# Triangular inverse in one group of eight matrices on VectorE and TensorE, in place of two groups of four

## The chip, the cores and the metric

The kernel runs on one core of a Trainium2 chip. TensorE (PE in the profile) does matrix products into PSUM, VectorE (DVE) and ScalarE (ACT) work on SBUF and PSUM, and the queue of SyncE (SP) loads weights. The metric is the device time of one execution in microseconds; the time before is the median of three runs.

## What is computed

The program is two layers of a hybrid decoder trunk on 256 tokens of 1024 channels: four parallel head groups (gated linear recurrence, gated DeltaNet, RG-LRU, RWKV-7), then cross-attention and a feed-forward part, which is SwiGLU in the first layer and eight experts in the second. The change touches the DeltaNet and RWKV groups alone. Each of them needs, once a layer, the inverses of unit triangular matrices that couple the tokens of a chunk. The kernel takes chunks of 128 tokens, so that with 4 heads and 256 tokens there are eight matrices of 128x128. For DeltaNet the reference has this system (with chunks of 64); for RWKV-7 it is the same kind of system, hidden in a scan over tokens:

```python
def chunk_gated_delta(q, k, v, g, beta):
    """S_t = exp(g_t)(I - b_t k_t k_t^T) S_{t-1} + b_t k_t v_t^T ; o_t = S_t^T q_t.
    q,k (B,H,S,dk), v (B,H,S,dv), g,beta (B,H,S)."""
    ...
    lower = jnp.einsum("bhntd,bhnsd->bhnts", kb, kc) * rel * strict
    rhs = jnp.concatenate([vc * bc[..., None], kb * jnp.exp(gc)[..., None]], axis=-1)
    uw = lax.linalg.triangular_solve(jnp.eye(CHUNK, dtype=f32) + lower, rhs,
                                     left_side=True, lower=True, unit_diagonal=True)
    ...
def rwkv7_scan(r, w, k, v, kk, a):
    """S_t = S_{t-1}(diag(w_t) - kk_t^T (a_t*kk_t)) + v_t^T k_t ; y_t = S_t r_t.  inputs (B,S,H,d)."""
```

## The kernel before

The program is written engine by engine: each engine has its own list of instructions, and semaphores (`wait_ge`, `then_inc`) are the only order between the lists. Each VectorE operation also waits for the one before it (`Chain`). `inverse(i)` stands once in VectorE's list and once in TensorE's. It runs four times: i = 0 (DeltaNet) and i = 1 (RWKV) in the first layer, i = 2 and 3 in the second. N holds the eight matrices side by side, 1024 columns. X and Y hold only their diagonal blocks of 64x64: the upper one on the first 64 partitions and the lower one on the others (`HALVES`), so that the eight matrices take 8 x 64 = 512 columns.

The inverse is built by doubling, in `LEVELS` = 7 levels v = 0 to 6. N is the triangular matrix, X its inverse so far and Y the transpose of X. In each level TensorE multiplies N and X into PSUM (T below), VectorE masks the result to the blocks of that level (T1), TensorE multiplies T1 with Y in both orders (P below), and VectorE subtracts the two from X and Y. Level 0 needs no P; level 5 keeps the upper half of the new Y in the columns from 512 on; level 6 makes the block that joins the two diagonal ones, with one product for each matrix where the levels below have two. The last copy of level 6 releases `solve`.

Before the change the eight matrices are handled as two groups of four (g = 0 and 1). Each group has its own PSUM banks (g, 2 + g, 4 + g) and its own counts on the semaphores `inv_t`, `inv_t1`, `inv_p` and `inv_xy`, whose target values come from `done_xy` and `done_p`.

Between the steps of a level other work is called by `after(v)`. On VectorE, in i = 0 and 2, this is `rwkv_ahead`: it prepares operands of the RWKV group at levels 0, 1, 3, 5 and 6 and stands between T1 and X. In i = 1 and 3 VectorE has no such work. On TensorE it is half of a memory-token projection (`kv`) at levels 0 and 1, one more product in i = 0 at level 1, and 8 transposes at level 3 in i = 1 (`turn_operands`); it stands behind P of its level.

All VectorE operations of a kind are recorded at the line of their helper: L812 for `tt`, L815 for `ts`, L1101 for the copy. TensorE's `mm` is L1462.

Of the kernel before, what the change touches and what calls it, by code (L numbers as in the profile page):

```python
# [103 lines left out]
def build(nc, A, out):  # L104
# [14 lines left out]
    with ExitStack() as ctx:  # L119
# [146 lines left out]
        def done_p(i, v, g, y):  # L266
            return (4 * LEVELS - 6) * i + 4 * (v - 1) + (2 * g + y + 1 if v < LEVELS - 1 else g + 1)
# [538 lines left out]
        def _(dve):  # L806
# [261 lines left out]
            def inverse(i, after=None):  # L1068


                N, X, Y, T1 = mt(3), mt(4), mt(5), mt(0)
                for v in range(LEVELS):
                    for g in range(2):
                        s_ = slice(256 * g, 256 * g + 256)
                        dve.wait_ge(S("inv_t"), 2 * (LEVELS * i + v) + g + 1)
                        if v == 0:
                            tt(many(T1[:, s_]), many(ps[:, g, 0:256]), rep(flip_b(0), 4), ALU.mult)
                            tt(many(X[:, s_]), rep(ident_b[:, :], 4), many(T1[:, s_]), ALU.subtract).then_inc(S("inv_xy"), 1)
                            for u in HALVES:
                                tt(many(T1[u, s_]), many(N[u, 512 * g:512 * g + 512])[:, :, u], rep(lvl(0)[u, u], 4), ALU.mult)  # L1080
                            tt(many(Y[:, s_]), rep(ident_b[:, :], 4), many(T1[:, s_]), ALU.subtract).then_inc(S("inv_xy"), 1)
                        elif v < LEVELS - 1:
                            tt(many(T1[:, s_]), many(ps[:, g, 0:256]), rep(flip_b(v), 4), ALU.mult).then_inc(S("inv_t1"), 1)
                        else:
                            ts(T1[HD:P, s_], ps[HD:P, g, 0:256], -1.0, ALU.mult).then_inc(S("inv_t1"), 1)
                    if after:
                        after(v)
                    if v:
                        for g in range(2):
                            s_ = slice(256 * g, 256 * g + 256)  # L1090
                            if v < LEVELS - 1:
# [366 lines left out]
        def _(pe):  # L1458
# [197 lines left out]
            def inverse(i, after=None):  # L1656
# [458 lines left out]
```

## Time and profile before

| what | value |
|---|---|
| median of 3 runs | 2117.27 us (2116.48 to 2118.86) |
| the profiled execution | 2117.68 us, span 2115.8 us |
| TensorE busy | 1922.4 us, 91% |
| VectorE busy | 1480.4 us, 70%, 1565 instructions |
| ScalarE busy | 1143.3 us, 54% |
| granted TensorE clock, mean | 0.941 |

The busy shares are means over stages with very different limits. The four inverses lie at about 205 to 244, 269 to 301, 830 to 869 and 894 to 928 us from the start of the span. In a timeline a row stands for one instruction or a run of like ones: its start, the time it covers, engine, line, operands, count, and in brackets how long the engine had been idle and what released it.

### The profile page before, as it was taken

To read this page: it belongs to the slowest core of one execution; us is meant where nothing else is said; L and a number is where in the kernel's file an instruction comes from. 1 tells how busy PE (TensorE), PEld (TensorE's weight loads), DVE (VectorE), ACT (ScalarE), POOL (GpSimd) and SP (SyncE) were. 2 spreads that over 40 slices of the span, in tenths; PEclk is the share of its full clock that TensorE was granted. 3 is DMA by queue.
4 is the path that set the end of the run, shared out by engine and by line. 5 is a ranking of instruction groups with operands and counts; after the bars stand their busy time and mean duration, and the time that the engine had idled before them with its cause. 6 is when DMAs were issued, how large, how long until landed. Compare 5 with 4: busy or idle time off the path is not lost.

```text
span 2115.8 us, 28844 instructions
## 1 busy us (share of the span) xinstructions
PE 1922.4 (91%) x12072; PEld 1637.5 (77%) x12073; DVE 1480.4 (70%) x1565; ACT 1143.3 (54%) x1078; POOL 0.2 (0%) x4
## 2 busy tenths in 40 slices
PE   6987789889998987789869999999999999999996
PEld 6975677779997966578748888888888888888884
DVE  6776544354447686535369888889888898988885
ACT  5543304343434643214357777767777776777773
POOL 0000000000000000000000000000000000000000
PEclk9997789989998998789979999999999999999998
DMA  7531003235554530003249999999999999999992
GB/s 227 173 127 40 22 22 113 86 114 189 193 193 123 179 102 22 20 22 120 80 157 384 346 358 338 378 334 368 355 337 364 333 387 328 369 357 340 358 374 83
DMA packets 238774, 466.06 MB, mean 220 GB/s; under 512 B 11056, under 2 KB 87088, under 8 KB 238640
## 3 DMA queue, kind: packets, MB, share of 16 engines
q1 hardware_dynamic: 238640, 464.16, 61.8%
q8 instruction: 97, 1.59, 0.3%
q14 instruction: 37, 0.30, 0.0%
HBM read 463.09 MB, written 1.05 MB: 219 GB/s over the span
## 4 chain that ended last, share of the span: by engine, by line
PE 83%; DVE 12%; ACT 3%; issue 2%; DVEq 0%; DMA 0%; ACTq 0%
PE ps L1887 29%; PE ps L1477 16%; PE ps L1897 14%; PE ps L1462 11%; PE ps L1495 7%; DVE MT L812 4%; PE ps L1943 1%; PE ps L1957 1%; PE ps L1918 1%; PE ps L1465 1%; DVE MT L815 1%; DVE hT_lo L818 1%; DVE TMP L812 1%; DVE MT L1032 1%; DVE MT L818 1%
## 5 line engine op out<-in xcount | busy, mean ns | idle before, releaser
L1253 DVE TENSOR_TENSOR wlo<-raw,whi 128x2048 fp32r<-128x2048 f32 x140 | 320.2, 2290 | 70.7 <-ACT whi L694 70.6
L694 ACT ACTIVATE whi<-raw 128x2048 fp32r<-128x2048 f32 x140 | 268.8, 1921 | 130.8 <-PE ps L1897 77.6
L825 DVE TENSOR_TENSOR wlo<-raw,whi 128x2048 fp32r<-128x2048 f32 x85 | 194.5, 2289 | 131.8 <-ACT whi L429 131.7
L1253 DVE TENSOR_TENSOR wlo<-PT,whi 128x2048 fp32r<-128x2048 f32 x84 | 192.1, 2291 | 33.6 <-ACT whi L694 33.6
L429 ACT ACTIVATE whi<-raw 128x2048 fp32r<-128x2048 f32 x85 | 161.9, 1905 | 55.9 <-PE ps L1495 46.7
L1887 PE MATMUL ps<-whi,hE_hi 128*128 128x512 f32 x672 | 185.4, 398 | 2.4 <-DVE hE_lo L1319 2.4
L694 ACT ACTIVATE whi<-PT 128x2048 fp32r<-128x2048 f32 x84 | 161.4, 1922 | 34.7 <-PE ps L1887 34.0
L1887 PE MATMUL ps<-wlo,hE_hi 128*128 128x512 f32 x672 | 180.1, 390 | 0.0
L1887 PE MATMUL ps<-whi,hE_lo 128*128 128x512 f32 x672 | 179.8, 389 | 0.0
L1477 PE MATMUL ps<-hT_hi,whi 128*128 128x256 f32 x928 | 136.3, 291 | 23.2 <-DVE hT_lo L818 23.2
L1887 PEld LDWEIGHTS ps<-wlo,hE_hi 128*128 128x128 f32 x672 | 126.2, 188 | 27.1
L1887 PEld LDWEIGHTS ps<-whi,hE_lo 128*128 128x128 f32 x672 | 126.2, 188 | 26.7
L1477 PEld LDWEIGHTS ps<-hT_hi,whi 128*128 128x128 f32 x928 | 124.8, 199 | 25.8 <-DVE hT_lo L818 24.9
L1887 PEld LDWEIGHTS ps<-whi,hE_hi 128*128 128x128 f32 x672 | 122.0, 188 | 24.8 <-DVE hE_lo L1319 2.6
L1897 PE MATMUL ps<-whi,act_hi 128*128 128x512 f32 x336 | 133.8, 398 | 1.4 <-DVE act_lo L1297 1.4
L1477 PE MATMUL ps<-hT_hi,wlo 128*128 128x256 f32 x928 | 134.2, 289 | 0.0
L1477 PE MATMUL ps<-hT_lo,whi 128*128 128x256 f32 x928 | 133.1, 287 | 0.0
L1897 PE MATMUL ps<-whi,act_lo 128*128 128x512 f32 x336 | 131.0, 390 | 0.0
L1897 PE MATMUL ps<-wlo,act_hi 128*128 128x512 f32 x336 | 130.7, 389 | 0.0
L1477 PEld LDWEIGHTS ps<-hT_hi,wlo 128*128 128x128 f32 x928 | 123.7, 198 | 0.0
L1477 PEld LDWEIGHTS ps<-hT_lo,whi 128*128 128x128 f32 x928 | 122.8, 197 | 0.0
L1462 PE MATMUL ps<-MT 64*64 64x64 f32 (+1 forms) x2272 | 90.4, 227 | 26.3 <-DVE MT L812 20.4
(259 smaller groups left out, 3313.9 us busy)
## 6 DMA issues: line engine op xcount, KB each, us to landing
raw<-in_moe_w_up SPq DMA_DIRECT2D x111, 1024.0 KB, 6.8
PT<-in_moe_w_down SPq DMA_DIRECT2D x56, 1024.0 KB, 6.5
PT<-in_moe_w_gate SPq DMA_DIRECT2D x55, 1024.0 KB, 6.7
TMP<-in_moe_w_gate SPq DMA_DIRECT2D x55, 1024.0 KB, 6.7
raw<-in_moe_w_down SPq DMA_DIRECT2D x55, 1024.0 KB, 6.4
raw<-in_w_in SPq DMA_DIRECT2D x28, 1024.0 KB, 5.5
raw<-in_ffn_w_gate SPq DMA_DIRECT2D x11, 1024.0 KB, 5.3
raw<-in_ffn_w_up SPq DMA_DIRECT2D x11, 1024.0 KB, 5.4
```

The lines of the kernel that those rows point to most:

```text
L429: nc.scalar.activation(whi[i % SPL][:, :], raw[d % RAW][:, :], ACT.Copy).then_inc(S("w_hi"), 1)
L694: nc.scalar.activation(ex_hi[m % XSPL], ex_raw[m % XRAW], ACT.Copy).then_inc(S("w_hi"), 1)
L812: return chain.link(lambda: V.tensor_tensor(o, x0, x1, op))
L815: return chain.link(lambda: V.tensor_scalar(o, x0, s1, s2, op0, op1) if op1 else V.tensor_scalar(o, x0, s1, None, op0))
L818: return chain.link(lambda: V.scalar_tensor_tensor(out=o, in0=x0, scalar=s_, in1=x1, op0=op0, op1=op1))
L825: V.tensor_tensor(wlo[i % SPL][:, :], raw[d % RAW][:, :], whi[i % SPL][:, :].bitcast(F32), ALU.subtract).then_inc(S("w_lo"), 1)
L1253: V.tensor_tensor(ex_lo[m % XSPL], ex_raw[m % XRAW], ex_hi[m % XSPL].bitcast(F32), ALU.subtract).then_inc(S("w_lo"), 1)
L1462: return Signalled(pe.matmul(o, lhsT, rhs, start=start, stop=stop, skip_group_check=True))
L1477: ins = pe.matmul(ps[:, bank, SEQ * m:SEQ * m + SEQ], wp[a_][:, k, P * m:P * m + P], src[b_][:, k, :], start=i == 0 and k == 0, stop=last)
L1495: ins = pe.matmul(ps[:, 4 + 2 * t + hf, :], src(b_, kk, t), wp[a_][:, kk, 512 * hf:512 * hf + 512], start=first and kk == 0 and i == 0, st ...
L1887: ins = pe.matmul(ps[:, bank, :], h_[b_][:, X_K * i + k, :], wp[a_][:, k, :], start=i == 0 and n_ == 0 and k == 0, stop=i == 1 and n_ == 2 ...
L1897: ins = pe.matmul(ps[:, 4 + hf, :], act_[b_][:, P * (TM_ROWS * i + kk):P * (TM_ROWS * i + kk) + P], wp[a_][:, kk, 512 * hf:512 * hf + 512] ...
```

## The change

The two groups become one. VectorE handles all eight matrices in one operation: 128x512 elements where there were two of 128x256. TensorE makes a product for all eight matrices before it signals, 16 matmuls of the program where it was 8 (at level 6, 8 where it was 4). The trace shows each of these fp32 matmuls as two. Banks 1, 3 and 5 are no longer used by the inverse, and the counts of the semaphores are halved. The number of matmuls is the same. Nothing else is touched.

```diff
-        def done_xy(i, v, g, y):
-            return (4 * LEVELS - 2) * i + 4 * v + (2 * g + y + 1 if v < LEVELS - 1 else g + 1)
+        def done_xy(i, v, y):
+            return (2 * LEVELS - 1) * i + 2 * v + (y + 1 if v < LEVELS - 1 else 1)
...
+                eight = lambda m: many(m[:, 0:512], 8)
                 for v in range(LEVELS):
-                    for g in range(2):
-                        s_ = slice(256 * g, 256 * g + 256)
-                        dve.wait_ge(S("inv_t"), 2 * (LEVELS * i + v) + g + 1)
-                        if v == 0:
-                            tt(many(T1[:, s_]), many(ps[:, g, 0:256]), rep(flip_b(0), 4), ALU.mult)
...
-                        elif v < LEVELS - 1:
-                            tt(many(T1[:, s_]), many(ps[:, g, 0:256]), rep(flip_b(v), 4), ALU.mult).then_inc(S("inv_t1"), 1)
-                        else:
-                            ts(T1[HD:P, s_], ps[HD:P, g, 0:256], -1.0, ALU.mult).then_inc(S("inv_t1"), 1)
+                    dve.wait_ge(S("inv_t"), LEVELS * i + v + 1)
+                    if v == 0:
+                        tt(eight(T1), many(ps[:, 0, :], 8), rep(flip_b(0), 8), ALU.mult)
...
+                    elif v < LEVELS - 1:
+                        tt(eight(T1), many(ps[:, 0, :], 8), rep(flip_b(v), 8), ALU.mult).then_inc(S("inv_t1"), 1)
+                    else:
+                        ts(T1[HD:P, 0:512], ps[HD:P, 0, :], -1.0, ALU.mult).then_inc(S("inv_t1"), 1)
                     if after:
                         after(v)
                     if v:
-                        for g in range(2):
-                            s_ = slice(256 * g, 256 * g + 256)
-                            if v < LEVELS - 1:
-                                dve.wait_ge(S("inv_p"), done_p(i, v, g, 0))
-                                tt(X[:, s_], X[:, s_], ps[:, 2 + g, 0:256], ALU.subtract).then_inc(S("inv_xy"), 1)
-                            dve.wait_ge(S("inv_p"), done_p(i, v, g, 1))
-                            if v < LEVELS - 2:
-                                tt(Y[:, s_], Y[:, s_], ps[:, 4 + g, 0:256], ALU.subtract).then_inc(S("inv_xy"), 1)
...
+                        if v < LEVELS - 1:
+                            dve.wait_ge(S("inv_p"), done_p(i, v, 0))
+                            tt(X[:, 0:512], X[:, 0:512], ps[:, 2, :], ALU.subtract).then_inc(S("inv_xy"), 1)
+                        dve.wait_ge(S("inv_p"), done_p(i, v, 1))
+                        if v < LEVELS - 2:
+                            tt(Y[:, 0:512], Y[:, 0:512], ps[:, 4, :], ALU.subtract).then_inc(S("inv_xy"), 1)
...
                 for v in range(LEVELS - 1):
-                    for g in range(2):
...
-                        if v:
-                            pe.wait_ge(S("inv_xy"), done_xy(i, v - 1, g, 0))
-                        blocks(g, n_, x_ if v else (lambda u, k: ident[u, u]), g).then_inc(S("inv_t"), 1)
                     if v:
-                        for g in range(2):
...
-                            pe.wait_ge(S("inv_xy"), done_xy(i, v - 1, g, 1))
-                            pe.wait_ge(S("inv_t1"), 2 * ((LEVELS - 1) * i + v - 1) + g + 1)
-                            blocks(2 + g, y_, t_, g).then_inc(S("inv_p"), 1)
-                            blocks(4 + g, t_, y_, g).then_inc(S("inv_p"), 1)
+                        pe.wait_ge(S("inv_xy"), done_xy(i, v - 1, 0))
+                    blocks(0, n_, x_ if v else (lambda u, k: ident[u, u])).then_inc(S("inv_t"), 1)
+                    if v:
+                        pe.wait_ge(S("inv_xy"), done_xy(i, v - 1, 1))
+                        pe.wait_ge(S("inv_t1"), (LEVELS - 1) * i + v)
+                        blocks(2, y_, t_).then_inc(S("inv_p"), 1)
+                        blocks(4, t_, y_).then_inc(S("inv_p"), 1)
```

On VectorE, in i = 1 at level 1 and the start of level 2, the list was this before (con16b is the mask, so a row with it is T1; MT,ps rows are X and Y, and inv_t, inv_p are the signals of T and P):

```order
L812 TENSOR_TENSOR MT<-ps,con16b 128x256 [waits inv_xy,inv_t]
L812 TENSOR_TENSOR MT<-ps,con16b 128x256 [waits inv_t1,inv_t]
L812 TENSOR_TENSOR MT<-MT,ps 128x256 [waits inv_t1,inv_p]
L812 TENSOR_TENSOR MT<-MT,ps 128x256 [waits inv_xy,inv_p] x3
L812 TENSOR_TENSOR MT<-ps,con16b 128x256 [waits inv_xy,inv_t]
L812 TENSOR_TENSOR MT<-ps,con16b 128x256 [waits inv_t1,inv_t]
L812 TENSOR_TENSOR MT<-MT,ps 128x256 [waits inv_t1,inv_p]
```

and is this now:

```order
L812 TENSOR_TENSOR MT<-ps,con16b 128x512 [waits inv_xy,inv_t]
L812 TENSOR_TENSOR MT<-MT,ps 128x512 [waits inv_t1,inv_p]
L812 TENSOR_TENSOR MT<-MT,ps 128x512 [waits inv_xy,inv_p]
L812 TENSOR_TENSOR MT<-ps,con16b 128x512 [waits inv_xy,inv_t]
L812 TENSOR_TENSOR MT<-MT,ps 128x512 [waits inv_t1,inv_p]
```

A level had six operations and has three, and each now waits for the signal of the whole product.

On TensorE, in i = 0 at level 3, the rows before are the T products of the two groups (8 matmuls each, of which the first waits) and then P of the two groups (16 each):

```order
L1462 MATMUL ps<-MT 64x64 [waits inv_xy]
L1462 MATMUL ps<-MT 64x64 x7
L1462 MATMUL ps<-MT 64x64 [waits inv_xy]
L1462 MATMUL ps<-MT 64x64 x7
L1462 MATMUL ps<-MT 64x64 [waits inv_t1,inv_xy]
L1462 MATMUL ps<-MT 64x64 x15
L1462 MATMUL ps<-MT 64x64 [waits inv_t1,inv_xy]
L1462 MATMUL ps<-MT 64x64 x15
```

and now:

```order
L1459 MATMUL ps<-MT 64x64 [waits inv_xy]
L1459 MATMUL ps<-MT 64x64 x15
L1459 MATMUL ps<-MT 64x64 [waits inv_t1,inv_xy]
L1459 MATMUL ps<-MT 64x64 x31
```

The four starts became two: one run of 16 for T and one of 32 for P. The products of a second group, which stood between a group's T and its P, are gone.

On VectorE at the end of i = 0, levels 5 and 6 before `rwkv_ahead`(6), the list was:

```order
L812 TENSOR_TENSOR MT<-MT,ps 128x256 [waits dve_step,inv_p]
L812 TENSOR_TENSOR MT<-MT,ps 64x256 [waits inv_xy,inv_p]
L812 TENSOR_TENSOR MT<-MT,ps 64x256 [waits dve_step]
L812 TENSOR_TENSOR MT<-MT,ps 128x256 [waits inv_xy,inv_p]
L812 TENSOR_TENSOR MT<-MT,ps 64x256 [waits inv_xy,inv_p]
L812 TENSOR_TENSOR MT<-MT,ps 64x256 [waits dve_step]
L815 TENSOR_SCALAR MT<-ps 64x256 [waits inv_xy,inv_t]
L815 TENSOR_SCALAR MT<-ps 64x256 [waits inv_t1,inv_t]
```

and is now:

```order
L812 TENSOR_TENSOR MT<-MT,ps 128x512 [waits dve_step,inv_p]
L812 TENSOR_TENSOR MT<-MT,ps 64x512 [waits inv_xy,inv_p]
L812 TENSOR_TENSOR MT<-MT,ps 64x512 [waits dve_step]
L815 TENSOR_SCALAR MT<-ps 64x512 [waits inv_xy,inv_t]
```

Eight operations became four; X comes first in both, and T1 of level 6 (L815) last.

## Rows read from the trace of the kernel before

**Rows 1.** The page: busy time and share of the span by engine; chain that ended last.
```profile
PE 1922.4 (91%) x12072; PEld 1637.5 (77%) x12073; DVE 1480.4 (70%) x1565; ACT 1143.3 (54%) x1078; POOL 0.2 (0%) x4
...
PE 83%; DVE 12%; ACT 3%; issue 2%; DVEq 0%; DMA 0%; ACTq 0%
```

**Rows 2.** Windows of i = 0 and i = 1: length, busy us of each engine, clock.
```profile
205.50:244.40 38.90, 29.24 (x578) 25.66 (x578) 31.75 (x71) 11.97 (x24) 0.00 (x0) 0.90 0.09 29
269.40:301.40 32.00, 28.84 (x584) 25.64 (x584) 20.64 (x47) 1.79 (x3) 0.00 (x0) 0.95 0.11 36
```

**Rows 3.** Timeline of i = 1, levels 1 and 2: start, duration, what, idle before.
```profile
276.07 1.15 PE L1462 MATMUL ps<-MT 64*64 64x64 f32 x32
276.80 0.95 DVE L812 TENSOR_TENSOR MT<-ps,con16b 128x256 f32<-128x256 f32 x2 [1.37 <-PE ps L1462]
...
277.37 2.08 PE L1462 MATMUL ps<-MT 64*64 64x64 f32 x64 [0.15 <-DVE MT L812]
...
283.03 1.15 PE L1462 MATMUL ps<-MT 64*64 64x64 f32 x32
...
284.33 3.01 PE L1462 MATMUL ps<-MT 64*64 64x64 f32 x96 [0.15 <-DVE MT L812]
```

**Rows 4.** Chain of waits in i = 1, level 4: start, duration, what.
```profile
292.06 0.70 PE ps L1462 x16
...
292.78 0.43 DVE MT L812
...
294.88 0.44 DVE MT L812
295.32 0.14 issue
295.45 0.70 PE ps L1462 x16
```

**Rows 5.** Groups of VectorE instructions by shape: busy us, mean ns | idle.
```profile
L812 DVE TENSOR_TENSOR MT<-MT,ps 128x256 f32<-128x256 f32 x72 | 30.3, 421 | 12.5 <-PE ps L1462 6.2 <-DVE MT L812 0.5
...
L812 DVE TENSOR_TENSOR MT<-MT,ps 128x512 f32<-128x512 f32 x11 | 7.6, 688 | 82.2 <-PE ps L1477 82.2
...
L812 DVE TENSOR_TENSOR MT<-ps,con 128x512 f32<-128x512 f32 x4 | 2.8, 691 | 0.9 <-PE ps L1462 0.7
```

**Rows 6.** Timeline of i = 1, P(6) and the first products of `solve`.
```profile
299.75 1.18 PE L1462 MATMUL ps<-MT 64*64 64x64 f32 x16 [0.93 <-DVE MT L815]
...
301.44 1.97 PE L1462 MATMUL ps<-TMP,MT 128*128 128x64 f32 x8 [0.51 <-DVE MT L1101]
```

**Rows 7.** Timeline of i = 0: T(0), T(1), P(1), T(2), X(3), X(5), copies, `solve`.
```profile
205.54 1.73 PE L1462 MATMUL ps<-con,MT 64*64 64x64 f32 x32 [2.96 <-DVE MT L812]
...
211.87 1.15 PE L1462 MATMUL ps<-MT 64*64 64x64 f32 x32
...
213.29 2.08 PE L1462 MATMUL ps<-MT 64*64 64x64 f32 x64 [0.28 <-DVE MT L812]
...
219.81 1.15 PE L1462 MATMUL ps<-MT 64*64 64x64 f32 x32
...
226.51 2.00 DVE L812 TENSOR_TENSOR MT<-MT,ps 128x256 f32<-128x256 f32 x4
...
235.31 2.90 DVE L812 TENSOR_TENSOR MT<-MT,ps 128x256 f32<-128x256 f32 x6
...
243.44 0.94 DVE L1101 COPY MT<-ps 64x256 f32<-64x256 f32 x2
...
244.44 2.16 PE L1462 MATMUL ps<-TMP,MT 64*64 64x64 f32 x16 [4.37 <-DVE MT L1101]
```

**Rows 8.** Windows at the end of i = 0; the clock stands after the engines.
```profile
236.00:240.00 4.00, 2.25 (x32) 1.93 (x30) 3.48 (x8) 0.00 (x0) 0.00 (x0) 1.00 0.00 0
240.00:244.40 4.40, 0.07 (x2) 0.00 (x0) 3.93 (x10) 0.00 (x0) 0.00 (x0) 0.50 0.00 0
```

**Rows 9.** Timeline of i = 3: a pause of TensorE inside P(3).
```profile
915.28 1.15 PE L1462 MATMUL ps<-MT 64*64 64x64 f32 x31 [1.26 <-issue]
```

More of the change, by code:

```diff
@@ L261, in at_b, with done_p @@
             return par_ * 256 + t * P + c * HD
[L263 to L267 removed]
+        def done_xy(i, v, y):
+            return (2 * LEVELS - 1) * i + 2 * v + (y + 1 if v < LEVELS - 1 else 1)
+        def done_p(i, v, y):
+            return (2 * LEVELS - 3) * i + 2 * (v - 1) + (y + 1 if v < LEVELS - 1 else 1)
         def col(a, n=1):
@@ L1658, in inverse, with blocks @@
                 pe.wait_ge(S("inv_n"), i + 1)
-                def blocks(bank, lhsT, rhs, g):
-                    for k in range(4):
+                def blocks(bank, lhsT, rhs):
+                    for k in range(2 * NH):
                         for u in HALVES:
@@ L1665, in blocks @@
                     return ins
+                n_ = lambda u, k: N[u, P * k + u.start:P * k + u.stop]
+                x_ = lambda u, k: X[u, HD * k:HD * k + HD]
+                y_ = lambda u, k: Y[u, HD * k:HD * k + HD]
+                t_ = lambda u, k: T1[u, HD * k:HD * k + HD]
                 for v in range(LEVELS - 1):
-                    for g in range(2):
-                        n_ = lambda u, k: N[u, 512 * g + P * k + u.start:512 * g + P * k + u.stop]
-                        x_ = lambda u, k: X[u, 256 * g + HD * k:256 * g + HD * k + HD]
-                        if v:
-                            pe.wait_ge(S("inv_xy"), done_xy(i, v - 1, g, 0))
-                        blocks(g, n_, x_ if v else (lambda u, k: ident[u, u]), g).then_inc(S("inv_t"), 1)
@@ L1682, in inverse @@
+                    blocks(0, n_, x_ if v else (lambda u, k: ident[u, u])).then_inc(S("inv_t"), 1)
[4 more added lines that the diff above has]
+                        blocks(4, t_, y_).then_inc(S("inv_p"), 1)
                     if after:
                         after(v)
-                for g in range(2):
-                    pe.wait_ge(S("inv_xy"), done_xy(i, LEVELS - 2, g, 0))
-                    for k in range(4):
-                        mm(ps[HD:P, g, HD * k:HD * k + HD], N[0:HD, 512 * g + P * k + HD:512 * g + P * k + P],
-                           X[0:HD, 256 * g + HD * k:256 * g + HD * k + HD]).then_inc(S("inv_t"), 1 if k == 3 else 0)
@@ L1689, in inverse @@
-                for g in range(2):
-                    pe.wait_ge(S("inv_xy"), done_xy(i, LEVELS - 2, g, 1))
-                    pe.wait_ge(S("inv_t1"), 2 * ((LEVELS - 1) * i + LEVELS - 2) + g + 1)
-                    for k in range(4):
-                        s_ = slice(256 * g + HD * k, 256 * g + HD * k + HD)
-                        mm(ps[0:HD, 4 + g, HD * k:HD * k + HD], T1[HD:P, s_], Y[HD:P, s_]).then_inc(S("inv_p"), 1 if k == 3 else 0)
+                pe.wait_ge(S("inv_xy"), done_xy(i, LEVELS - 2, 0))
@@ new lines, in inverse @@
+                for k in range(2 * NH):
+                    mm(ps[HD:P, 0, HD * k:HD * k + HD], N[0:HD, P * k + HD:P * k + P],
+                       X[0:HD, HD * k:HD * k + HD]).then_inc(S("inv_t"), 1 if k == 2 * NH - 1 else 0)
+                pe.wait_ge(S("inv_xy"), done_xy(i, LEVELS - 2, 1))
+                pe.wait_ge(S("inv_t1"), (LEVELS - 1) * i + LEVELS - 1)
+                for k in range(2 * NH):
+                    s_ = slice(HD * k, HD * k + HD)
+                    mm(ps[0:HD, 4, s_], T1[HD:P, s_], Y[HD:P, s_]).then_inc(S("inv_p"), 1 if k == 2 * NH - 1 else 0)
@@ L1695, in inverse @@
                 if after:
                     after(LEVELS - 1)
[L1697 removed]
+                pe.wait_ge(S("inv_xy"), done_xy(i, LEVELS - 1, 0))
             def solve(bank, t, r_):
```

21 lines of the change are left out of this document (9 added, 12 removed).

## The prediction

> **What bounds the kernel now.** I read the busy shares and the chain of work that ended last first [rows 1]. TensorE holds 83% of the chain, VectorE 12%. That average says little about the inverse, so I asked for the busy time over the stretches of the two inverses of the first layer [rows 2]: i = 0 takes about 38.9 us, with VectorE busy for 31.75 and TensorE for 29.24; i = 1 takes about 32.0, with TensorE busy for 28.84 and VectorE for 20.64 only. The second pair, in the second layer, has the same instructions. So the four inverses are some 143 us of 2116, and in the odd ones VectorE is idle a third of the time: there its operations matter by their latency, not by their sum.
>
> Names below: T(v) are the products N·X of level v, T1(v) the VectorE operation that masks them, P(v) the two sets of products after it (first those for X, then those for Y), X(v) and Y(v) the two subtractions. A number after a colon is a start in the trace.
>
> The timeline of i = 1 shows the steps [rows 3]. T(1) starts at 276.07 with no idle time in front of it: it stood in TensorE's queue behind the memory-token products. T1(1) for the first four matrices starts 0.73 later, P(1) starts at 277.37, so T to P is 1.30. Level 2 repeats it: 283.03, again without idle time, then 284.33. The two groups overlap: while VectorE masks the first four matrices, TensorE makes the products of the other four. The trace has two matmuls for each product of the program, so a product of one group (8 blocks) is 16 matmuls. 96 in 3.01 against 32 in 1.15 give 29 ns for each, so 16 of them are 0.47 us.
>
> The chain of waits in level 4 shows the other case, with no foreign products in the way [rows 4]: P(4) at 292.06, 0.72 until X of the first group, then X, Y, X, Y at 0.525 each (292.78 to 294.88), T1 of the first group 0.44, a gap of 0.14, and P(5) at 295.45. The period is 3.39 us. T(5) is not in that chain at all: it lies under the four subtractions. The second T1 lies under the first products of P.
>
> **The change, part by part.** VectorE: an inverse had 10 operations at level 0, 6 in each of levels 1 to 4, 8 at level 5 and 4 at level 6, together 46; it has 5, 3 each, 4 and 2, together 23. That is 92 operations fewer in four inverses. A 128x256 one from PSUM takes 421 ns, a 128x512 one 688 to 691 [rows 5], so a pair of 0.84 becomes 0.69, and with the gaps 1.05 becomes 0.78. VectorE loses 92 x 0.155 = 14 us of busy time. I use 0.69 for every merged operation, since both rows at 512 columns have it, with and without a mask. No row has the bf16 mask at 512 columns, so the bounds are 0.69 and 0.84 (nothing gained over two).
>
> TensorE: the same matmuls, in runs of 32 of the trace's matmuls in place of 16. Every wait for a block now lasts 16 matmuls longer, 0.47 us: T to T1 becomes 0.73 + 0.47 = 1.20, P to X becomes 0.72 + 0.47 = 1.19.
>
> What each costs on the path:
> - T to P, where TensorE's queue sets the start of T: 1.20 + 0.69 + 0.14 = 2.03 in place of 1.30, **+0.73**. The cover that is gone is the second group's T products, under which the first T1 lay. In i = 1 this is levels 1 and 2 (memory-token products ahead) and level 4 (8 transposes ahead): 2.19 us.
> - A period with nothing foreign in it, from P(v) to P(v+1): 1.19 to X, 0.69 for X, 0.14, then T (the queue is free at 64 x 0.0294 = 1.88, so X at 2.02 decides), 1.20 to T1, 0.69, 0.14: 4.05 in place of 3.39, **+0.66**. Y(v) runs from 2.13 to 2.82, before T1 can start at 3.22: it is hidden. What was a chain of VectorE operations becomes a strict alternation of the engines. In i = 1 these are P(2) to P(3) and P(4) to P(5): 1.32 us.
> - The tail of i = 1, from P(5) at 295.45 to the first product of `solve` at 301.44 [rows 4, 6] is 5.99. After: P(5) lets X start at 1.19; the lower and upper Y (64x512, taken at 0.69 like a full one) follow at 2.13 and 2.86 and end at 3.55; the T1 of level 6 from 3.62 to 4.31 (T(6) is 16 matmuls at 65 ns, from the 16 in 1.18 of P(6) [rows 6], done by 3.3); P(6) at 4.45; the copy 1.20 later, at 5.65, 0.69 long; `solve` at 6.40: **+0.41**.
> An odd inverse therefore loses 2.19 + 1.32 + 0.41 = 3.92 us. Level 0 costs nothing there: its operations end before T(1), which the memory-token products hold back to 276.07.
>
> In i = 0 VectorE also does the work of `rwkv_ahead`, and parts of it are bound by VectorE. From [rows 7]: T(0) runs at 54 ns a matmul (32 in 1.73), so T1(0) waits 0.86 longer, and five operations of 0.73 in place of ten of 0.46 give that back. T(1) at 211.87 is set by the queue; P(1) comes 2.03 later, at 213.90 in place of 213.29. From there to T(2) TensorE is the limit (6.52 us from 213.29 to 219.81), so T(2) is at 220.42, P(2) at 222.45, P(3) at 226.50. T1(3) ends 0.14 before that; two operations of `rwkv_ahead` follow, 1.57 with their gaps: X(3) at 227.93, where it was 226.51: +1.42. From X(3) to X(5) it was 8.80. Now 0.69 + 0.14 + 1.20 + 0.69 + 0.14 = 2.86 to P(4), 4.05 to P(5), of which T1(5) ends 0.14 before, and three operations of `rwkv_ahead` with gaps, 2.31: 9.08, +0.28. From X(5) at 235.31 to `solve` at 244.44 VectorE works without a pause, 9.13. Of the inverse's ten operations in it five are left: X, Y, Y, T1 and the copy take 3.82 with their gaps, and `rwkv_ahead` 4.05 as before, 7.87 in all: -1.26. An even inverse therefore loses 1.42 + 0.28 - 1.26 = 0.44 us.
>
> The sum is 2 x (3.92 + 0.44) = 8.7 us. Everything after an inverse is a chain: `solve` waited for the last copy in both [rows 6, 7], and the chain of the whole run has no DMA share [rows 1], so I take the delay as passed on in full. The profiled execution took 2117.68 (its span is 2115.8), which gives 2126.4; against the median of 2117.27 it is 2126.0.
>
> **A rule against the rows.** The rows say that merging two operations saves 0.155 us of VectorE, and that it pays only where VectorE is the limit. The Trainium skill, "VectorE: DVE Perf Modes", section on the TRN2 errata, says that every Vector instruction pays a fixed latency and advises tiles of 512 elements or more so that it is paid once. The durations agree with it; followed alone it would take off up to the 14 us of busy time and speaks for a faster kernel. The rival of that name below is worked out from the rows.
>
> **The rivals.**
> - *VectorE stays the limit (faster).* If the next T were still hidden, a period would be two operations with gaps, T1, the gap and P to X: 0.78 + 0.78 + 0.69 + 0.14 + 1.19 = 3.58, still not under 3.39. To win, X must also start 0.72 after P: 3.11, 0.28 less. Over five levels of two odd inverses that is -2.8, with the two tails of the even ones -2.5: about 2112. The point that decides is whether T to T1 stays near 0.73 with twice the products, and [rows 3] show 29 ns a matmul, so 32 cannot be done by then. 5%.
> - *The loss is absorbed (same).* The odd loss of 3.9 passes on only if nothing later waits for something else. No DMA stands in the chain; but one stall of TensorE by its own instruction stream, 1.26 us before the products at 915.28 [rows 9], lies inside i = 3 and could vanish or fall on an idle stretch. With the stall gone (-1.3) and VectorE the limit at level 3 of the even inverses too, so that their loss of 0.44 turns into the whole gain of the tail (-1.26 each, 3.4 less for the two), it is 2121.3. 10%.
> - *The clock falls inside an inverse (slower still).* The granted clock stayed at 1.00 while TensorE was busy for 2.25 of 4.00 us, and stood at 0.50, which is 1.2 GHz, in the stretch after, in which it was idle [rows 8]. The new period leaves it busy for 2.8 of 4.05 us, a higher share than the 0.56 of that first row, so I expect no fall. If it did fall, matmuls at 54 ns [rows 7] make a period 6.3 us in place of 4.05, about 2.2 for each level until it rises: two such places in two inverses give +4 to +9, 2130 to 2135. The Trainium skill, "Perfetto Trace Analysis", section Matmul Optimizations, asks for matmuls back to back because the engine scales with use; this change takes that away in the odd inverses. 9%.
> - *The walk holds:* 76%, by itself 2122.5 to 2129.5: -1.3 for the stall, -1.2 to +1.6 for the spread of the three runs, +2 for half of the bound of 0.84 for a merged operation (two of them on the path of ten periods, 0.15 each, is 3 us).
>
> **The numbers.** The likeliest is 2126. With the stall, the spread and the two neighbours the range for 8 in 10 is 2121 to 2130.5. A measurement can tell 0.2%, 4.2 us, from no change: below 2113 is faster, above 2121.5 slower. Slower takes the walk and the clock, 85%; same 10%; faster 5%.
>
> **What would show it.** VectorE busy near 1466 in place of 1480 us; matmul count unchanged. In i = 1 the distance from P(4) to P(5) near 4.05, with VectorE idle before T1 for some 0.4 us and before X for some 0.4; T to P near 2.03; the stretch of i = 1 near 36 us and that of i = 0 near 39.3. In i = 0 `solve` should follow X(5) by 7.9. The prediction is wrong if merged operations take well over 0.69, if TensorE issues the wider blocks faster than 29 ns a matmul, or if the clock row of an inverse shows 0.5 where it was 1.0.

## The result and the profile after

| | before | after |
|---|---|---|
| median (range), 5 runs each on one chip | 2118.68 us (2116.48 to 2118.94) | 2127.07 us (2126.59 to 2128.49) |
| span of the profiled execution | 2115.8 us | 2124.7 us |
| VectorE busy | 1480.4 us, 1565 instructions | 1466.5 us, 1473 instructions |

The ratio is 1.0044, with a 95% interval from 1.0029 to 1.0059: 8.4 us slower by the medians. The forecast was 8.7 slower. In the kernel after, the helpers stand three lines higher: `mm` is L1459 and the copy L1098.

The page of after answers to [rows 1]: first the busy times, then the chain of work that ended last.

```profile
PE 1924.4 (91%) x12072; PEld 1640.7 (77%) x12073; DVE 1466.5 (69%) x1473; ACT 1143.3 (54%) x1078; POOL 0.2 (0%) x4
...
PE 85%; DVE 10%; ACT 3%; issue 1%; DVEq 0%; DMA 0%; ACTq 0%
```

VectorE lost 92 instructions and 13.9 us of work, the number of matmuls is the same, and the kernel is slower all the same. In the chain of work that ended last, VectorE's share went from 12% to 10% and TensorE's from 83% to 85%: of the blocks of matmuls that VectorE's work used to cover, more now lie on the path.

The windows of after's first two inverses, cut at their own first T(0) and first product of `solve`, answer to [rows 2] (length, busy time of each engine, clock):

```profile
203.98:243.54 39.56, 29.67 (x579) 26.31 (x579) 28.20 (x48) 11.97 (x24) 0.00 (x0) 0.89 0.09 28
268.55:304.24 35.69, 29.08 (x585) 26.18 (x585) 17.07 (x24) 1.79 (x3) 0.00 (x0) 0.93 0.10 32
```

In i = 1 VectorE does 17.07 us of work where it did 20.64, in 24 operations where it had 47. TensorE does the same work. The window is 3.7 us longer: both engines now stand idle more.

The timeline of after in i = 1 shows where (start, duration, what, idle before and its releaser). It answers to [rows 3, 4, 6]:

```profile
275.04 1.15 PE L1459 MATMUL ps<-MT 64*64 64x64 f32 x32
276.24 0.69 DVE L812 TENSOR_TENSOR MT<-ps,con16b 128x512 f32<-128x512 f32 x1 [2.08 <-PE ps L1459]
277.07 2.08 PE L1459 MATMUL ps<-MT 64*64 64x64 f32 x64 [0.89 <-DVE MT L812]
...
293.80 3.08 PE L1459 MATMUL ps<-MT 64*64 64x64 f32 x96 [0.89 <-DVE MT L812]
294.99 0.69 DVE L812 TENSOR_TENSOR MT<-MT,ps 128x512 f32<-128x512 f32 x1 [1.33 <-PE ps L1459]
295.92 0.69 DVE L812 TENSOR_TENSOR MT<-MT,ps 128x512 f32<-128x512 f32 x1 [0.25 <-PE ps L1459]
296.93 0.69 DVE L812 TENSOR_TENSOR MT<-ps,con16b 128x512 f32<-128x512 f32 x1 [0.32 <-PE ps L1459]
297.76 3.07 PE L1459 MATMUL ps<-MT 64*64 64x64 f32 x80 [0.89 <-DVE MT L812]
298.95 0.69 DVE L812 TENSOR_TENSOR MT<-MT,ps 128x512 f32<-128x512 f32 x1 [1.33 <-PE ps L1459]
...
302.24 1.22 PE L1459 MATMUL ps<-MT 64*64 64x64 f32 x16 [1.40 <-DVE MT L815]
303.50 0.68 DVE L1098 COPY MT<-ps 64x512 f32<-64x512 f32 x1 [1.41 <-PE ps L1459]
304.24 1.97 PE L1459 MATMUL ps<-TMP,MT 128*128 128x64 f32 x8 [0.78 <-DVE MT L1098]
```

Read the brackets. TensorE stands 0.89 us before each of P(1) to P(5), released by T1, where it stood 0.15 before P(1), P(2) and P(4) [rows 3] and 0.38 before P(3) and P(5). VectorE stands 0.32 us before T1, 0.25 before Y and 1.33 before X. T to P is 277.07 - 275.04 = 2.03 us (it was 1.30), the period P(4) to P(5) 3.96 (3.39), and from P(5) to `solve` 6.48 (5.99).

In i = 0 the rows of after that answer to [rows 7] are X(5) with the two Y behind it, the copy and `solve`:

```profile
235.63 2.20 DVE L812 TENSOR_TENSOR MT<-MT,ps 128x512 f32<-128x512 f32 x3
...
242.80 0.68 DVE L1098 COPY MT<-ps 64x512 f32<-64x512 f32 x1
243.54 2.16 PE L1459 MATMUL ps<-TMP,MT 64*64 64x64 f32 x16 [2.83 <-DVE MT L1098]
```

From X(5) to `solve`, 235.63 to 243.54, it is 7.91 us in place of 9.13. This is the one place that gained.

### The profile page after: what moved, and what is told of

The parts are those of the page before. It is cut to its first block, busy times and chain, and to the rows that moved or that the text cites. A ratio compares the mean times of both kernels' runs of the same rounds, so it can differ in the third digit from the quotient of the medians.

```text
span 2124.7 us, 28656 instructions
## 1 busy us (share of the span) xinstructions
PE 1924.4 (91%) x12072; PEld 1640.7 (77%) x12073; DVE 1466.5 (69%) x1473; ACT 1143.3 (54%) x1078; POOL 0.2 (0%) x4
## 4 chain that ended last, share of the span: by engine, by line
PE 85%; DVE 10%; ACT 3%; issue 1%; DVEq 0%; DMA 0%; ACTq 0%
PE ps L1880 29%; PE ps L1474 16%; PE ps L1890 14%; PE ps L1459 13%; PE ps L1492 7%; DVE MT L812 3%; PE ps L1936 1%; PE ps L1950 1%; PE ps L1911 1%; PE ps L1462 1%; DVE hT_lo L818 1%; DVE TMP L812 1%; DVE MT L815 1%; DVE MT L1032 1%; ACT L420 1%
## 5 line engine op out<-in xcount | busy, mean ns | idle before, releaser
L1459 PE MATMUL ps<-MT 64*64 64x64 f32 (+1 forms) x2272 | 90.2, 228 | 35.1 <-DVE MT L812 29.6
```

What stands on the lines that cost most here:

```text
L1459: return Signalled(pe.matmul(o, lhsT, rhs, start=start, stop=stop, skip_group_check=True))
```

## The measure used below

I cut each trace at the first T(0) of an inverse and at the first product of `solve` after it. The lengths in us, for every kernel that ran; the numbers in brackets run from T(1) instead, and so leave out level 0. The last column is the sum of the four inverses. "Ahead" and "filled" name kernels with products that nobody reads; all are explained at their experiments.

| kernel | i = 0 | i = 1 | i = 2 | i = 3 | four |
|---|---|---|---|---|---|
| before | 38.90 (32.57) | 32.00 (25.37) | 39.07 (32.77) | 33.59 (26.87) | 143.56 |
| before, second trace | 39.10 (32.80) | 32.06 (25.36) | 38.99 (32.68) | 33.55 (27.03) | 143.70 |
| after | 39.55 (33.24) | 35.69 (29.20) | 39.15 (32.88) | 35.70 (29.08) | 150.09 |
| after, second trace | 39.54 (33.25) | 35.67 (29.22) | 39.16 (32.88) | 35.70 (29.08) | 150.07 |
| odd merged | 38.84 (32.51) | 35.75 (29.08) | 39.10 (32.80) | 35.78 (29.08) | 149.47 |
| even merged | 39.55 (33.24) | 32.56 (26.06) | 39.19 (32.88) | 33.30 (26.61) | 144.60 |
| T merged | 42.08 (35.76) | 36.41 (29.75) | 41.65 (35.40) | 37.06 (30.39) | 157.20 |
| X, Y merged | 38.08 (31.77) | 32.05 (26.50) | 38.00 (31.70) | 33.01 (27.46) | 141.14 |
| tail merged | 37.92 (31.62) | 30.94 (25.36) | 37.88 (31.58) | 32.57 (26.96) | 139.31 |
| mixed | 37.82 (31.51) | 31.14 (25.48) | 37.43 (31.12) | 31.89 (26.91) | 138.28 |
| before, 32 products ahead | 38.82 (32.49) | 33.21 (26.55) | 39.02 (32.71) | 31.85 (25.36) | 142.90 |
| before, 16 products ahead | 38.94 (32.62) | 31.95 (25.36) | 39.06 (32.75) | 31.80 (25.36) | 141.75 |
| before, idle stretch filled | 38.86 (32.53) | 32.68 (26.01) | 39.16 (32.91) | 32.19 (25.53) | 142.89 |
| mixed, idle stretch filled | 37.78 (31.47) | 31.54 (25.85) | 37.46 (31.14) | 30.92 (25.94) | 137.70 |

Outside the inverses the same instructions ran in all of them, and yet these parts differ from trace to trace: up to the first T(0) 202.4 to 205.7 us, between the layers' inverses 528.8 to 532.0, behind the last one 1186.3 to 1189.3. A change of some 3 us in one span therefore says nothing of the inverse; the table does.

## The experiments

The kernels of experiments take the number of groups from two functions, and the counts of the semaphores from tables built with them:

```python
def groups_t(i, v): return 2      # groups of T and T1 in inverse i, level v
def groups_x(i, v): return 2      # groups of P, X and Y
```

With 2 and 2 the two lists are ordered as before, with 1 and 1 as after. In these kernels `tt` stands at L837, the copy at L1129 and `mm` at L1490.

### The two kernels again

No edit: before and after ran once more beside the later kernels, for a second trace of each.

> The kernel before once more, for a second trace. If the pause of TensorE of 1.26 us inside P(3) of i = 3 belongs to the program, it is there again at the same instruction and i = 3 takes 33.6 from T(0) to solve; if it is chance, i = 3 takes 32.0 like i = 1 and the true loss of i = 3 by the change is 3.7 and not 2.11. The stretches outside the inverses (head to T(0) of i = 0; solve of i = 1 to T(0) of i = 2; solve of i = 3 to the end) should differ from the first trace by up to 2 us, as the granted clock rises and falls at other moments.

> The changed kernel once more. T(0) to solve 39.5, 35.7, 39.2, 35.7 again within 0.3 if these are fixed by the chain of instructions. The stretches outside the inverses, which gave +0.9 +1.5 -1.5 us against the first trace of before, scatter by 2 us if they are chance; if they stay, the change costs something behind the inverses as well.

Measured: 2119.26 us and 2126.44 us, spans 2117.3 and 2124.6. The four inverses repeat within 0.2 us each; i = 3 of before has its pause again, at the same matmul and 0.98 us long. The spans differ by 7.3 where the first two differ by 8.9. What the inverses say is thus known to some tenths, and what lies outside them to one or two us.

### Merging the odd or the even inverses alone

```diff
-            return 2      # both functions
+            return 1 if i % 2 else 2      # odd; the other kernel has 2 and 1 exchanged
```

> One group of eight in i = 1 and 3 only, two groups of four in i = 0 and 2. Theory (a block of 32 matmuls has to be waited for where it was hidden, and only where VectorE has no other work does that cost much): the whole loss stands here, 2 x 3.9 by the prediction and 3.69 + 2.11 in the traces, so 6 to 8 us slower than the kernel before, ratio 1.003 to 1.0037. From T(0) to solve: 35.7 in i = 1 and 3, 38.9 to 39.1 in i = 0 and 2. Rival (the loss is not in the inverses but in the granted clock or waits behind them, where the two traces also differ by 2 to 4 us): the distances from T(0) to solve explain less than half of the change of the median, or the ratio is below 1.002.

> One group of eight in i = 0 and 2 only. Theory: loss in levels 1 to 4 and gain in the tail cancel, +0.4 each by the prediction, +0.65 and +0.08 in the traces: within 0 to +1.5 us of the kernel before, ratio 1.000 to 1.0007. T(0) to solve near 39.5 in i = 0 and 39.2 in i = 2, 32.0 in i = 1 and 3 (33.6 with the pause of TensorE). Rival (VectorE is the limit in the even inverses, so 23 operations fewer must pay 23 x 0.155 = 3.6 us each): 7 us faster, ratio 0.9966.

Measured: odd merged 2125.12 us, ratio 1.0028 (1.0017 to 1.0039); even merged 2120.14, ratio 1.0008 (0.9999 to 1.0017); before on the same chip 2119.01. The odd inverses carry most of the loss (the medians move by 6.1 us, the inverses of the table by 5.9), and the even ones are almost neutral, as the walk has it. With the even ones merged, they are +0.65 and +0.12 against a forecast of 0.44 each. The same trace shows how far an inverse moves without an edit: i = 1 is 0.7 longer from T(1) on, all of it in level 6, and the granted clock over its last 2.0 us was 0.66, where it was 1.00 in before.

### Merging one side of the exchange

The next two kernels take the change apart. One merges T and T1 and leaves P, X and Y in two groups, the other does the reverse:

```diff
 def groups_t(i, v):
-    return 2
+    return 1      # T merged
 def groups_x(i, v):
-    return 2
+    return 1      # X, Y merged (groups_t stays at 2)
```

If the long operations were what costs, the second would lose, since it holds most of them. If it is the wait for a whole block of T, the first must lose everything, or more, because it pays the wait and keeps VectorE's four subtractions.

> T and its mask in one group of eight, P and the subtractions X and Y in two groups of four. Theory: T(v+1) must wait for the X of both groups and T1 for all of T, so a period with nothing foreign in it is X, Y, X (0.72 + 1.05 + 0.43), 0.14, T 1.20, T1 0.69, 0.14 = 4.37, more than the 4.05 with everything merged though VectorE has more but shorter operations; T to P 2.03. Odd inverses 32.0 + 4.5 = 36.5, even ones 38.9 + 2.9 = 41.8; sum +15 us against the kernel before, ratio 1.007. Rival (what costs is the long operation itself, since a 128x512 subtraction holds back X and Y): two thirds of the long operations are gone, so the loss is smaller than that of the full change, under 8 us.

> T and its mask in two groups of four, P and the subtractions in one group of eight. Theory: with T in two groups T1 of the first starts 0.73 after T again, so T to P is 1.30 as before; a period is 1.19 to X, 0.69, Y from 2.13 to 2.82, T1 at 2.90, 0.43, 0.14 = 3.47 (3.39 before, 4.05 with everything merged). Odd inverses +0.9, of which 0.65 in the tail, near 32.9; even ones -1.4, near 37.5; sum -1 us against the kernel before, ratio 0.9995, and 9 us faster than the full change. Rival (every merged wait costs, not that on T alone): half of the loss of the full change stays, +4 us, ratio 1.002.

Measured: T merged 2133.48 us, ratio 1.0071 (1.0057 to 1.0084), slower than the full change. X and Y merged 2113.78, ratio 0.9978 (0.9969 to 0.9987), faster than before.

The timeline of T merged in i = 1, levels 2 and 3:

```profile
286.27 2.08 PE L1490 MATMUL ps<-MT 64*64 64x64 f32 x64 [0.89 <-DVE MT L837]
286.99 2.00 DVE L837 TENSOR_TENSOR MT<-MT,ps 128x256 f32<-128x256 f32 x4 [0.86 <-PE ps L1490]
288.51 1.15 PE L1490 MATMUL ps<-MT 64*64 64x64 f32 x32 [0.16 <-DVE MT L837]
289.71 0.69 DVE L837 TENSOR_TENSOR MT<-ps,con16b 128x512 f32<-128x512 f32 x1 [0.72 <-PE ps L1490]
...
290.55 2.08 PE L1490 MATMUL ps<-MT 64*64 64x64 f32 x64 [0.89 <-DVE MT L837]
```

The four subtractions start 0.72 after P, as before, but TensorE can begin the merged T only behind the second X; the period is 290.55 - 286.27 = 4.28 us. The timeline of X, Y merged, level 4:

```profile
287.60 1.15 PE L1490 MATMUL ps<-MT 64*64 64x64 f32 x32
288.33 0.95 DVE L837 TENSOR_TENSOR MT<-ps,con16b 128x256 f32<-128x256 f32 x2 [0.96 <-PE ps L1490]
...
288.90 3.14 PE L1490 MATMUL ps<-MT 64*64 64x64 f32 x96
290.15 0.69 DVE L837 TENSOR_TENSOR MT<-MT,ps 128x512 f32<-128x512 f32 x1 [0.86 <-PE ps L1490]
...
291.87 0.95 DVE L837 TENSOR_TENSOR MT<-ps,con16b 128x256 f32<-128x256 f32 x2
...
292.44 3.13 PE L1490 MATMUL ps<-MT 64*64 64x64 f32 x80 [0.40 <-DVE MT L837]
```

T to P is 1.30, as before, and the period 3.54, 0.15 over the 3.39 of before: the subtractions are those of after, 0.69 long, and cost nearly nothing. So it is the block of T that VectorE must wait for, and then the whole T1 that TensorE must wait for. The merged subtractions themselves are not dear.

X, Y merged came out better than expected, but not by its merge. From T(1) on its odd inverses lose 1.1 and 0.6 us, and the even ones gain 0.8 and 1.1 (forecast 1.4): together -0.2 us. Level 0, T(0) to T(1), is 1.1 shorter in both odd inverses, which no step of the inverse explains; it has the same instructions as before. The rows of TensorE there, first of before and then of the mixed kernel (below), which has the same gain, show what it is:

```profile
269.44 1.15 PE L1462 MATMUL ps<-con,MT 64*64 64x64 f32 x32 [1.95 <-DVE MT L818]
270.77 5.37 PE L1462 MATMUL ps<-raw,memT 128*128 128x256 f32 x16 [0.18 <-DVE PT L818]
276.07 1.15 PE L1462 MATMUL ps<-MT 64*64 64x64 f32 x32
```

```profile
267.79 1.97 PE L1490 MATMUL ps<-con,MT 64*64 64x64 f32 x32 [0.22 <-DVE MT L843]
269.69 3.82 PE L1490 MATMUL ps<-raw,memT 128*128 128x256 f32 x16
273.45 1.15 PE L1490 MATMUL ps<-MT 64*64 64x64 f32 x32
```

The same 16 memory-token matmuls take 5.37 us in one and 3.82 in the other, and T(0) is the slower one in the second. The windows of the granted clock over 264 to 270 and 270 to 276 us, before and then mixed, agree (the clock stands third from the end):

```profile
264.00:270.00 6.00, 2.61 (x50) 2.42 (x52) 5.50 (x7) 0.00 (x0) 0.00 (x0) 1.00 0.00 0
270.00:276.00 6.00, 5.82 (x37) 4.61 (x32) 4.94 (x11) 0.00 (x0) 0.00 (x0) 0.72 0.01 3
```

```profile
264.00:270.00 6.00, 5.78 (x65) 5.37 (x66) 5.54 (x6) 0.00 (x0) 0.00 (x0) 0.51 0.01 3
270.00:276.00 6.00, 5.85 (x91) 5.05 (x92) 4.72 (x13) 0.00 (x0) 0.00 (x0) 1.00 0.00 0
```

A stretch at 0.50 (1.2 GHz) lies over the memory-token products in before, and ahead of them in the mixed kernel. There it costs nothing: from `solve` to the next T(0) it is 25.0 us in both. This is where the microsecond comes from. The four inverses of X, Y merged together are 2.4 us shorter than in before, of which 2.25 are these two levels 0; the medians are 5.2 apart, and what the remainder outside the inverses is, one trace can't tell.

### Merging only where VectorE is the limit

In even inverses the tail is bound by VectorE. The first kernel merges there T of level 6 and P, X, Y of levels 5 and 6, the second also P, X and Y of levels 3 and 4:

```diff
 def groups_t(i, v):
-    return 2
+    return 1 if i % 2 == 0 and v == LEVELS - 1 else 2
 def groups_x(i, v):
-    return 2
+    return 1 if i % 2 == 0 and v >= LEVELS - 2 else 2      # tail; mixed: v >= 3
```

> The kernel before, with one group of eight only in i = 0 and 2 and there only from P(5) on: P, X and Y of level 5, and all of level 6. Theory: this is the part of the change in which VectorE works without a pause, -1.26 in each of two inverses, T(0) to solve 37.6 and 37.8, odd ones as before: -2.5 us, ratio 0.9988. Rival (the wait for the wider products eats it here too): 0.

> As the run with the merged tail, and in i = 0 and 2 also P, X and Y of levels 3 and 4 in one group of eight (T and T1 stay in two groups). Theory: from X(3) to P(4) 2.13 in place of 2.68, the period of level 4 3.47 in place of 3.39, then the tail: -1.7 in each even inverse, 37.2; -3.4 us, ratio 0.9984. Rival (at level 3 the wait for P decides, not VectorE): no more than the merged tail alone, -2.5 us.

Measured: tail merged 2115.65 us, ratio 0.9986 (0.9976 to 0.9995); mixed 2112.30, ratio 0.9970 (0.9958 to 0.9982), against 2118.65 for before. The tail gives -1.0 and -1.2 in the even inverses, where the forecast's term is -1.26. Mixed gives -1.1 and -1.6 there, where -1.7 each was expected. Both have the clock's microsecond in the odd inverses on top. From T(1) on, so without level 0, the four inverses together are 2.1 us (tail) and 2.6 us (mixed) shorter than in before. That is what these merges gave; of the 6.4 us by which the median of mixed is lower, more than half is not their work. Mixed has the lowest median here, though its interval overlaps that of X, Y merged.

### Is the pause in i = 3 tied to its place?

Merging cost 3.69 us in i = 1 but 2.11 in i = 3, because before has a pause of TensorE in i = 3 [rows 9] that after has not. The bracket of the pause names only issue, no other engine. If it comes from how the list of instructions is supplied, then moving the list by some instructions must move or remove it. So I put products that nobody reads ahead of everything else in TensorE's list, at its very start:

```diff
 pe.wait_ge(S("tables_in"), 32)
+for k in range(32):      # 16 in the other kernel
+    u = HALVES[k % 2]
+    mm(ps[u, 7, HD * (k % 8):HD * (k % 8) + HD], ident[u, u], ident[u, u])
```

> The kernel before with 32 extra 64x64 products at the start of TensorE's list, while it waits for the input (they write a bank that is written again later, so they cost no time of their own). They only move every later instruction of TensorE further along its list. Theory (the pause in P(3) of i = 3, 1.26 and 0.98 us in two traces, comes from TensorE's supply of instructions, which arrive in pieces, and matmuls of 29 ns use them up faster than they come): the pause moves to another place, about two products of 32 matmuls earlier, or disappears under a wait; where it disappears i = 3 falls from T(1) to solve from 26.9 to 25.4, and the kernel is about 1.5 us faster, ratio 0.9993. Rival (the pause belongs to this place of the program, for instance to the product that meets another engine's access there): it stays at the second half of P(3), T(1) to solve 26.9.

> The same with 16 extra products. Theory of supply: the pause stands about 32 of the trace's matmuls earlier than in the kernel before, near the end of T(3) or the first half of P(3), in i = 3, and likewise in i = 0. Rival: it does not move.

Measured: 32 products 2116.91 us, ratio 0.9999 (0.9990 to 1.0008), with before at 2118.10, so the 1.5 us expected did not show; 16 products 2114.29 in one run, where runs of before went from 2114.8 to 2120.4. The timeline of TensorE in i = 1 with 32 products:

```profile
281.16 3.02 PE L1462 MATMUL ps<-MT 64*64 64x64 f32 x96 [0.15 <-DVE MT L812]
284.54 1.38 PE L1462 MATMUL ps<-MT 64*64 64x64 f32 x40 [0.37 <-DVE MT L812]
286.70 0.91 PE L1462 MATMUL ps<-MT 64*64 64x64 f32 x24 [0.78 <-issue]
```

and with 16:

```profile
284.12 3.02 PE L1462 MATMUL ps<-MT 64*64 64x64 f32 x96 [0.15 <-DVE MT L812]
287.51 2.08 PE L1462 MATMUL ps<-MT 64*64 64x64 f32 x64 [0.38 <-DVE MT L812]
```

With 32 the pause has left i = 3 and split P(3) of i = 1 into 40 and 24, with 0.78 between; with 16 neither odd inverse has one, where a pause some 32 matmuls earlier was expected. Where there is none, T(1) to `solve` is 25.36 in i = 1 and i = 3 alike. From 25.36 the merge costs 3.72 us in i = 3, against 3.83 in i = 1.

The filled kernel of the next experiment bears on this too. It has 24 extra products ahead of i = 1, which the trace shows as 48 matmuls, and this pause:

```profile
287.77 1.85 PE L1462 MATMUL ps<-MT 64*64 64x64 f32 x56 [0.38 <-DVE MT L812]
290.05 0.45 PE L1462 MATMUL ps<-MT 64*64 64x64 f32 x8 [0.43 <-issue]
```

With 64 matmuls more in the list (the 32 products) the pause stands behind the 40th of P(3), with 48 more behind the 56th: both are the same place of the list, 104 matmuls behind where P(3) starts in before. So the pause goes with the position in the list, and not with a place of the program. Both traces of before also have one of 0.64 in P(3) of i = 0, at the same matmul; it costs nothing, since without it T(1) to `solve` is 32.49 and 32.62 in place of 32.57: VectorE sets the pace there.

### Can the idle stretch ahead of `solve` be filled?

Tail and mixed have a shorter idle stretch of TensorE ahead of `solve` in i = 0, and the clock comes back earlier behind it. If the idle stretch is the reason, products that nobody reads put there must bring the same in before:

```diff
+                if i % 2 == 0:      # behind P(6)
+                    for k in range(24):
+                        u = HALVES[k % 2]
+                        mm(ps[u, 1, HD * (k % 8):HD * (k % 8) + HD], ident[u, u], ident[u, u])
```

> The kernel before with 24 products of 64x64 that nobody reads, issued by TensorE in i = 0 and 2 behind P(6), where it is idle for 4.4 us until solve. No wait and no VectorE operation changes. In the three kernels with a shorter even inverse, T(0) to T(1) of the odd inverse behind it took 5.0 to 5.7 us and the low clock ended 3 to 4 us earlier; in all others it took 6.4 to 6.7. Theory (how long TensorE stood idle in front of solve sets when the granted clock comes back, and so the time of the memory-token products in the next inverse): with the idle time cut to about 2 to 3 us, T(0) to T(1) of i = 1 and 3 falls to 5.5 as well, and the kernel is 2 us faster, ratio 0.999; no change in T(0) to solve of i = 0 and 2. Rival (it is the earlier start of what follows, or chance): T(0) to T(1) stays at 6.4 to 6.7.

> The mixed kernel (i = 0 and 2: X and Y of levels 3 to 5 and all of level 6 in one group of eight) with the same 24 products behind P(6). Its idle time in front of solve is 2.8 us or so already, and with the products about 1 us. If the idle time sets the clock, the low stretch after i = 0 becomes shorter again and the kernel falls below the mixed one, 2110 to 2112; if not, it stays at 2112.3, or is slower by up to 1 us where the extra products at the lower clock run into solve.

Measured: filled 2114.90 us, ratio 0.9980 (0.9971 to 0.9989); mixed and filled 2114.04, ratio 0.9976 (0.9967 to 0.9986), no better than mixed. The idle time ahead of `solve` did shrink, from 4.37 [rows 7] to 2.26:

```profile
244.44 2.15 PE L1462 MATMUL ps<-TMP,MT 64*64 64x64 f32 x16 [2.26 <-DVE MT L1101]
```

but T(0) to T(1) is 6.67 and 6.66 in the odd inverses, as in before (6.63 and 6.72). The memory-token products of i = 1 took 5.41 again:

```profile
270.77 5.41 PE L1462 MATMUL ps<-raw,memT 128*128 128x256 f32 x16 [0.18 <-DVE PT L818]
```

So the expectation fails: T(0) to T(1) did not shorten, and the idle time ahead of `solve` does not by itself decide when the clock comes back. But in one of the four places of the two kernels it did come back. These are the first products of `solve` in i = 2, before and then filled; the granted clock over them is 0.50 in the first and 1.00 in the second:

```profile
869.47 2.16 PE L1462 MATMUL ps<-TMP,MT 64*64 64x64 f32 x16 [4.09 <-DVE MT L1101]
```

```profile
873.25 1.28 PE L1462 MATMUL ps<-TMP,MT 64*64 64x64 f32 x16 [1.73 <-DVE MT L1101]
```

It was at 0.50 again from 875 us on, and the stretch from this `solve` to T(0) of i = 3 is 0.86 us shorter for it. For the rest, i = 3 is 1.4 us shorter with its pause all but gone (the list is longer by these products), and i = 1 is 0.7 longer with its pause of 0.43. The 3.65 us between the medians is not told by this: the profiled execution took 2117.94, the slowest of its eleven, and is no faster than before.

## Why the prediction was right, point by point

The mechanism is the one forecast; the total is nearer than its terms.

- **T to P, +0.73.** Exact: 2.03 us at T(1), T(2) and T(4) of i = 1. The cover that went was the second group's T, as X, Y merged shows by keeping it and keeping 1.30.
- **A period, +0.66.** Measured +0.57 (3.96 us). The step from X to the next T was mis-sized: I let T wait for X and a gap of 0.14, but T follows P in one unbroken run of 96 matmuls, since X ends just as the products of Y do. It is 0.09 less in each of two periods.
- **The tail of an odd inverse, +0.41.** Measured +0.49: P(6) to the copy took 1.26 and P(5) to P(6) 4.48, against 1.20 and 4.45. In i = 3 of after P(5) to `solve` is 6.36, against the 6.40 of the forecast.
- **Odd inverse, +3.92.** T(1) to `solve` of i = 1 is 3.83 longer (25.37 to 29.20). In i = 3 the trace shows 2.21 only, because the pause of [rows 9] is gone. The forecast had this pause in its range and in its rival *absorbed*, and not in its sum. Measured from 25.36 the merge itself costs 3.72.
- **Even inverse, +0.44.** Measured +0.65 and +0.08 in the first pair of traces, +0.44 and +0.17 in the second. In i = 0 the gain is as forecast, `solve` 7.91 behind X(5) (forecast 7.87). The loss ahead of it was mis-sized: +1.73 from T(0) to X(3), where the forecast has 1.42, and +0.14 from there to X(5), where it has 0.28. P(3) to X(3) took 1.84 in place of the forecast's 1.43, because VectorE stood 0.46 between T1(3) and the first operation of `rwkv_ahead`:

```profile
224.01 0.69 DVE L812 TENSOR_TENSOR MT<-ps,con16b 128x512 f32<-128x512 f32 x1 [0.32 <-PE ps L1459]
225.16 1.42 DVE L812 TENSOR_TENSOR MT<-MT,PT 128x512 f32<-128x512 f32 x2 [0.46 <-DVE MT L812]
226.69 1.48 DVE L812 TENSOR_TENSOR MT<-MT,ps 128x512 f32<-128x512 f32 x2
```

- **The whole.** The four inverses gave +6.53 us in the first pair of traces and +6.37 in the second, not 8.7. Of the 2.2 that are missing 1.5 are the pause in i = 3 (26.87 with it, 25.36 without). The medians moved by 8.4, of which thus some 2 lie outside the inverses, in stretches with unchanged instructions (in the first pair -1.55 up to the first T(0), +2.40 between the layers, +1.51 at the end). So the total agrees better than the sum behind it deserves, and that is luck: the 2.2 by which the sum was too high were made up by some 2 us outside the inverses, which the forecast has at nothing. Whether a part of that is scatter or a lasting shift of the clock's stretches is not settled (the end is 1.5 and 1.2 longer in the two pairs); for odd merged the medians moved by 6.1 and the inverses by 5.9.
- **The range.** 2126 less 1.3 and 1.2 is 2123.5, where the forecast of the walk has 2122.5, and half of its bound of 3 us is 1.5, where it has 2. The measured 2127.07 lies inside by either.
- **VectorE idle before X, 0.4.** Wrong as a marker: it is 1.33. By the prediction's own walk it had to be: T1 ends 0.14 before P, and X starts 1.19 behind P. The 0.25 in the trace stands before Y.
- **VectorE stays the limit (5%).** False, by the 0.89 us that TensorE waits for each T1. The rule of the Trainium skill, "VectorE: DVE Perf Modes", section on the TRN2 errata, on operations of 512 elements or more, is right on busy time (13.9 us less), though its heading speaks of operations that read SBUF and T1 reads PSUM here; and the time did not follow it, except in the even tails (-1.0 and -1.2).
- **The clock falls inside an inverse (9%).** Not in levels 1 to 5. In i = 0 it fell ahead of P(6) and not behind it, so that P(6) took 1.93 us in place of 1.18, but `solve` waited for the last copy at 242.80 and P(6) had ended at 240.71. The window of after at that place, for [rows 8]:

```profile
236.00:240.00 4.00, 2.36 (x28) 2.26 (x29) 3.65 (x7) 0.00 (x0) 0.00 (x0) 0.78 0.00 0
```

## What to carry to other kernels

Where two engines hand work back and forth, as in this inverse, two groups are not overhead but the cover: price a merged operation by the wait for the other engine's whole block (here T to P became 0.73 us longer), and not only by the 0.155 that it saves. Merge where the trace shows the engine without idle time (here P, X and Y from level 3 on in the even inverses), and leave the rest split: from T(1) on that made the four inverses 2.6 us shorter, where merging everything made them 6.8 longer. The ratio of 0.9970 is larger than these 2.6 us, and 24 products that nobody reads, with nothing merged, gave 0.9980. So compare the stretch that was edited, over two traces, before trusting that the whole moved for the reason given.

## What the runs showed of the hardware

- TensorE's list of small matmuls (29 ns each) has pauses of 0.2 to 1.3 us in the inverses for which the profile names no other engine. They go with the position in the list: of the odd inverses i = 3 had one in P(3), with 32 products more at the start i = 1 had one in its P(3) instead (and i = 2 one of 0.54), and with 16 more neither had. With 64 and with 48 matmuls more ahead of it, the pause in i = 1 stood at the same place of the list. That this is the supply of instructions fits, but no run shows the supply itself. No trace of a kernel with T merged in the odd inverses (after twice, odd merged, T merged) shows one there; that the waits of 0.89 us in each level hide it is argued, not shown (i = 3 of T merged is 0.64 longer than its i = 1, which is not explained).
- The granted clock has stretches at 0.50 whose place shifts with small edits. Level 0 of an odd inverse, the same instructions each time, took 5.0 to 5.7 us in all eight odd inverses of the four kernels that merge X and Y of the even tail and keep T of levels 1 to 5 in two groups (X, Y merged, tail merged, mixed, mixed and filled), and 6.4 to 6.7 in all the others. It is worth about 1 us for each odd inverse (1.7 in i = 3 of mixed). What brings it about is open: filling the idle stretch ahead of `solve` did not shorten level 0 in any of the four places, and raised the clock over the first products of `solve` in one of them.
